# Two feed-forward stages of a two-block layer stack: sums of activations made while gate/up runs, two loads a step, and another sharing out of the norm's work

## The reference

```python
for layer in range(DEPTH):                       # DEPTH = 2
    h = rms_norm(hs, norm_mix_pre[layer])
    mix = pool_mixer(h, ...) if layer < N_A_LAYERS else sliding_window_attention(h, ...)
    hs = hs + rms_norm(mix, norm_mix_post[layer])
    h = rms_norm(hs, norm_ffn_pre[layer])
    gate, up = jnp.split(h @ w_gate_up[layer], 2, axis=-1)
    hs = hs + rms_norm((jax.nn.silu(gate) * up) @ w_down[layer], norm_ffn_post[layer])
# after layer 0: kv_in = rms_norm(hs, kv_norm), keys and values from it
# second_block: h = x * (1 + scale) + shift, then h @ w_in and the rest
```

## Time and profile before

| | us |
|---|---|
| median of 3 runs (range) | 2718.04 (2714.65 to 2721.75) |
| profiled execution | 2723.42 |
| its span | 2721.7 |
| PE busy | 2486.6 (91% of the span) |
| DVE busy | 1529.2 (56%) |
| ACT busy | 1004.8 (37%) |
| POOL busy | 239.8 (9%) |
| f0: down from 569.84 to 823.90, then the norm's rest to | 847.38 |
| f1: down from 1659.65 to 1909.86, then the norm's rest to | 1937.77 |

### The profile page before, as it was taken

How to read it: one execution, slowest core, us unless ns; L and a number is a source line. 1 busy time by engine, 2 the same in 40 slices (tenths; PEclk the granted TensorE clock), 3 DMA queues, 4 the chain that set the end, 5 groups by cost and what they waited for, 6 DMA issues and landing times. The chain is left out here.

```text
span 2721.7 us, 49445 instructions
## 1 busy us (share of the span) xinstructions
PE 2486.6 (91%) x20201; PEld 2066.5 (76%) x20201; DVE 1529.2 (56%) x2352; ACT 1004.8 (37%) x1787; POOL 239.8 (9%) x173
## 2 busy tenths in 40 slices
PE   9899999999977999989999999897799998788778
PEld 7889999987766856667888888685577776677556
DVE  5844454447764558467555554777344563455366
ACT  5433233334444259343323233343221512233231
POOL 2000000001011035100000000002310000222110
PEclk9899999999988999999999999998799999899879
DMA  6423323257444400332222225644212112000132
GB/s 173 118 81 110 108 89 112 97 175 231 138 159 160 186 5 2 101 108 89 82 81 81 81 77 188 236 148 143 97 58 77 39 62 91 4 5 4 57 109 97
DMA packets 122867, 276.15 MB, mean 101 GB/s; under 512 B 17237, under 2 KB 25718, under 8 KB 121150
## 3 DMA queue, kind: packets, MB, share of 16 engines
q1 hardware_dynamic: 122688, 273.60, 30.3%
HBM read 219.68 MB, written 53.28 MB: 100 GB/s over the span
## 5 line engine op out<-in xcount | busy, mean ns | idle before, releaser
L1391 PE MATMUL f1ps<-f1ring 128*128 128x512 f32 x308 | 123.7, 402 | 21.5 <-DVE f1ring L1245 12.9
L1391 PE MATMUL f0ps<-f0ring 128*128 128x512 f32 x308 | 124.9, 406 | 19.3 <-DVE f0ring L1245 13.0
L1392 PE MATMUL f0ps<-f0ring 128*128 128x512 f32 x308 | 122.6, 398 | 0.0
L1393 PE MATMUL f0ps<-f0ring 128*128 128x512 f32 x308 | 122.6, 398 | 0.0
L1392 PE MATMUL f1ps<-f1ring 128*128 128x512 f32 x308 | 122.1, 396 | 0.0
L1393 PE MATMUL f1ps<-f1ring 128*128 128x512 f32 x308 | 122.0, 396 | 0.0
L1287 PE MATMUL f0ps<-b1XH,f0highE 128*128 128x260 f32 x384 | 111.2, 289 | 4.1 <-DVE f0lowE L1112 4.1
L1638 PE MATMUL w_in_b_pr<-b1XH,w_in_b_wH 128*128 128x512 f32 x272 | 110.5, 406 | 3.6 <-DVE w_in_b_wL L1590 3.6
L1169 DVE TENSOR_TENSOR Y_rounded<-Y,Y_rounded 128x1024 fp32r<-128x1024 f32 x80 | 87.1, 1089 | 46.2 <-ACT Y_rounded L971 46.1
L1288 PE MATMUL f0ps<-b1XL,f0highE 128*128 128x260 f32 x384 | 109.6, 285 | 0.0
L1289 PE MATMUL f0ps<-b1XH,f0lowE 128*128 128x260 f32 x384 | 109.6, 285 | 0.0
(11 more groups left out here) (524 smaller groups left out, 7699.4 us busy)
## 6 DMA issues: line engine op xcount, KB each, us to landing
b1XL_plain<-in_w_down SPq DMA_DIRECT2D x66, 256.0 KB, 3.0
residual<-Y SPq DMA_DIRECT2D x32, 512.0 KB, 2.9
Y<-in_w_ada SPq DMA_DIRECT2D x8, 1536.0 KB, 6.5
f0hidden<-f0tm SPq DMA_DIRECT2D x44, 260.0 KB, 4.6
Y<-in_w_gate_up SPq DMA_DIRECT2D x44, 256.0 KB, 2.8
Y<-in_w_gate_up SPq DMA_DIRECT2D x22, 512.0 KB, 3.3
f0ring_plain<-f0hidden SPq DMA_DIRECT2D x44, 256.0 KB, 2.9
f1hidden<-f1tm SPq DMA_DIRECT2D x44, 256.0 KB, 3.0
```

What stands on the lines that cost most here:

```text
L1391: pe.matmul(o, ah, bh, start=fresh, stop=False, skip_group_check=True)
L1392: pe.matmul(o, ah, bl, start=False, stop=False, skip_group_check=True)
L1393: return pe.matmul(o, al, bh, start=False, stop=last, skip_group_check=True)
```

## The change

- **Sums of activations.** While gate/up runs, VectorE makes four sums of the halves of each pair of chunks, and SP stores seven tiles a pair in place of four, each 128x512 (`hidden` now has eight kinds: A11, A12, A22, A21 and SUM1 to SUM4). The pair of plain chunks gets its sums in the down stage: four tiles are loaded back after the last gate/up store, summed before step 9 and stored before step 15.
- **Down.** Every step has exactly two loads. VectorE makes one sum a step in P5, P6, P7 and P4 and none in the others: 44 in place of 88 an FFN. P1 and P5 are rounded in one operation 1024 wide. R is 6, and four steps are loaded before gate/up ends (BEFORE = 4). SP issues step 4's loads behind the store of the last SUM4 (`store_last`), which waits for `pair_last` on VectorE and must have landed.
- **Norm.** VectorE adds the residual behind the multiplication by the gain (L631 after); GpSimd has no part in it. ScalarE issues the stores and the further residual loads (`keep_and_load`). Gains, first weights and first residual tiles are loaded one after the other over steps P6_FIRST + 1 to + 10. A tile's operations come at other steps of P7 and P4. In f1 TensorE turns the residual sum itself, and ScalarE applies scale and shift to the turned tile, eight operations 128x128 with one number per partition for each of both (L596), and then copies the high part (L599).
- **Meta tokens (f0).** They are split over both halves; GpSimd copies them together with four small operations a pair of chunks.

```diff
-    R = 5
+    R = 6
+    BEFORE = 4
...
-                "P1": [(ra, hidden_tiles(j, 0)), (kb, down(j, 0)), (sa, hidden_tiles(j, 1))],
-                "P5": [(sa, hidden_tiles(j, 1)), (ks, hidden_tiles(k2, 1)), (sb, down(j, 1))],
-                "P6": [(sa, down(k2, 1))],
-                "P3": [(ra, hidden_tiles(k2, 0)), (rb, down(k2, 1))],
-                "P7": [(sa, down(j, 0))],
...
+                "P1": [(ca, hidden(A11, j)), (cb, down(low_q, 0))],
+                "P5": [(ca, hidden(SUM1, j)), (rb, down(low_q, 1))],
+                "P6": [(ra, hidden(SUM2, j)), (rb, down(high_q, 1))],
+                "P3": [(ra, hidden(SUM4, j)), (rb, down(high_q, 1))],
+                "P7": [(ra, hidden(SUM3, j)), (rb, down(low_q, 0))],
...
+                def store_last(m):
+                    sp.wait_ge(s["hs"], 4 * m + 4)
+                    sp.dma_start(hidden(SUM4, m + 1), sequence(tm[:, 1, 1])).then_inc(s_ss[2], 16)
...
+                for k, kind in enumerate((A11, A21, A12, A22)):
+                    sp.dma_start(z[:, k], hidden(kind, 0)).then_inc(s_z, 16)
+                store_last(PAIRS - 1)
...
+                for k in range(3):
+                    sp.wait_ge(s_ss[k], 16 * PAIRS)
...
+                def pair_difference(i, m):
+                    dve.wait_ge(s["h"], 2 * i + 6)
+                    dve.tensor_tensor(tm[:, 0, 3], tm[:, 0, 1], tm[:, 0, 2], ALU.subtract).then_inc(s["hs"], 1)
+
+                def pair_sums(i, m):
+                    dve.wait_ge(s["h"], 2 * i + 8)
+                    dve.tensor_tensor(tm[:, 1, 0], tm[:, 0, 2], tm[:, 1, 2], ALU.add).then_inc(s["hs"], 1)
+                    dve.wait_ge(s["hs"], 4 * m + 2)
+                    dve.tensor_tensor(tm[:, 1, 3], tm[:, 1, 0], tm[:, 0, 1], ALU.subtract).then_inc(s["hs"], 1)
+
+                def pair_last(m):
+                    dve.wait_ge(s_st[1][0], 16 * (m + 1))
...
+                    dve.wait_ge(s["hs"], 4 * m + 3)
+                    dve.tensor_tensor(tm[:, 1, 1], tm[:, 1, 1], tm[:, 1, 3], ALU.subtract).then_inc(s["hs"], 1)
...
+                def keep_and_load(t):
+                    tail.keep(act, t)
+                    if t + tail.loads < tail.N:
+                        tail.load(act, t + tail.loads)
...
+                if self.modulate:
+                    for k in range(f.start, f.stop):
+                        act.activation(self.xn[:, t % 2, P * k:P * (k + 1)], self.tp[:, t % self.slots, k, 0:r], ACT.Identity,
+                                       bias=self.shift[:, k:k + 1], scale=self.scale[:, k:k + 1]).then_inc(s["xf"], 1)
+                    act.wait_ge(s["xf"], KC * t + f.stop)
...
-        first_at = {AT + 3 * i: t for i, t in enumerate(TOP)}
-        second_at = {AT + 2 + 3 * i: t for i, t in enumerate(TOP)}
...
+        act_first = {AT + 3 * i: t for i, t in enumerate(TOP)}
+        dve_first = {AT + 1 + 3 * i: t for i, t in enumerate(TOP)}
+        act_second = {AT + 2 + 3 * i: t for i, t in enumerate(TOP)}
+        dve_second = {AT + 3 + 3 * i: t for i, t in enumerate(TOP)}
...
+        load_at = {P6_FIRST + 4 + 2 * t: t for t in range(tail.loads)}
```

More of the change, by code:

```diff
@@ L674, in strassen_ffn @@
     wdn = ins["w_down"][layer]
-    h_out = nc.dram_tensor(name + "hidden", [P, NQ, 2 * half], f32, kind="Internal").ap()
+    h_out = nc.dram_tensor(name + "hidden", [P, 8, HQ, 512], f32, kind="Internal").ap()
+    A11, A12, A22, A21, SUM1, SUM2, SUM3, SUM4 = range(8)
     fetched = 16 * b.fetched
@@ L881, in body @@
                         fetch_down(i + 3, 1)
-                    before = (0 if first else 1 - par)
-                    store(i + 1, before, 0, 2 * (i + 1))
-                    store(i + 1, before, 1, 2 * (i + 1))
+                    if first:
+                        store_classical(1, 0)
+                        store_classical(1, 1)
+                    elif par == 0:
+                        store_odd(i - 1, m - 1)
+                    else:
+                        store_even(i - 1, m)
                     if more:
@@ L889, in body @@
                         fetch_c(i + 4, par)
+                    if par == 0 and not first:
+                        store_last(m - 1)
                 for k in range(2):
@@ L931, in _ @@
-                store(NQ - 1, 1, 0, 2 * NQ - 2)
-                store(NQ - 1, 1, 1, 2 * NQ - 2)
+                body(N - 1, 1, PAIRS - 1, more=False)
                 sp.wait_ge(s["prod"], 7 * N)
-                for par in range(2):
-                    for i in range(2):
-                        sp.wait_ge(s_st[par][i], 16 * (N // 2 + (2 if par == 0 else 0)))
-                if off:
-                    sp.wait_ge(s["meta"], N // 2 + 2)
-                kept = 0
-                for n in range(R - 1, len(steps)):
-                    if n == P6_FIRST - 2:
+                store_odd(N - 1, PAIRS - 1)
@@ L942, in _ @@
+                for n in range(BEFORE, len(steps)):
+                    if n == P1_FIRST + 4:
+                        sp.wait_ge(s["zs"], 4)
+                        for k, kind in ((1, SUM1), (3, SUM2), (4, SUM3), (2, SUM4)):
+                            sp.dma_start(hidden(kind, 0), z[:, k]).then_inc(s_z, 16)
+                    if n == P5_FIRST:
+                        sp.wait_ge(s_z, 128)
+                    step_loads(n)
+                    if n == P6_FIRST + 1:
                         fetch(sp)
+                    if n == P6_FIRST + 2:
@@ L943, in _ @@
                         tail.load_gains(sp)
-                        for t in range(tail.loads):
-                            tail.load(sp, t)
-                    step_loads(n)
-                    if n in keep_at:
-                        tail.keep(sp, kept)
-                        tail.load(sp, kept + tail.loads)
-                        kept += 1
-                for t in range(kept, tail.N):
-                    tail.keep(sp, t)
-                    if t + tail.loads < tail.N:
-                        tail.load(sp, t + tail.loads)
+                    if n in load_at:
+                        tail.load(sp, load_at[n])
@@ L1024, in body @@
                     else:
-                        for n in range(R - 1):
+                        for n in range(BEFORE):
                             step_high(n)
@@ L1077, in _ @@
                 done = {P1_FIRST + AHEAD: (P1_FIRST - 1, bank_b, 0, 0), P6_FIRST + AHEAD: (P6_FIRST - 1, bank_b, 1, 1), P3_FIRST + AHEAD: (P3_FIRST - 1, bank_a, 0, 1)}
-                for n in range(R - 1, len(steps)):
+                for n in range(BEFORE, len(steps)):
                     if n in done:
                         copies(*done[n])
-                    if off and n == R + 2:
+                    if off and n == 7:
                         act.wait_ge(s["meta"], N // 2 + 2)
@@ L1182, in body @@
                     dve.tensor_tensor(tm[:, par, 1], tm[:, par, 1], group(C_GROUP), ALU.add).then_inc(s["c"], 1)
+                    if par == 0 and pair:
+                        pair_last(m - 1)
                     if more:
@@ L1270, in run @@
                         step_low(n)
+                    for n in sorted(low_at):
+                        if n >= len(steps):
+                            tail.vector_low(dve, low_at[n])
                     for k in range(7):
```

319 lines of the change are left out of this document (196 added, 123 removed).

## The result

The changed kernel takes 2675.23 us (median of 4, 2670.3 to 2683.32) against 2717.89: ratio .9845, 95% interval .9816 to .9875. A second set of runs gave 2671.25 against 2722.01, ratio .9816 (.9794 to .9839). So it is 1.5 to 1.8% faster, 43 to 51 us; 2683 was forecast, a gain of 35.

What follows compares the result with a forecast made beforehand. Gate/up was taken as bound by TensorE, down as losing time to stalls in P5, P6, P7 and P4. Terms 0 + 12.4 - 23.7 - 31.0 + 6.8 = -35.5 gave 2683 us, range 2658 to 2707.

Steps and rivals of the forecast that it cites:

- P1: Down product P1 of both FFNs: no change in time, 0 us.
- P7 and P4: Down products beside the norm's operations: fewer PE stalls, -31.0 us, as -14.1 in f0 and -16.9 in f1.
- Gate/up: Gate/up stage: four added VectorE sums a pair of chunks hidden in waits for PE, 0 us; bounds 0 and +56.
- Start of down: P2, down's start: step 4's loads wait for SUM4's store to land, +12.4 us (f1 +7.4, f0 +5.0).
- P5 and P6: Down products P5 and P6: two loads a step, spread burst and fewer sums remove all stalls, -23.7 us.
- Norm behind P4: Norm's rest after P4: +6.8 us, as +6.5 in f0 (addition 4.8, ScalarE's stores 1.7) and +0.3 in f1.
- B: Rival: ScalarE and VectorE in lockstep stall P7 and P4 much as before; +21, 2704 us; chance .16.
- E: Rival: loads late again in P5 to P4, three quarters of 23.7 stays; +18, 2701 us; chance .10.
- D: Rival: gate/up sums wait for a landing and delay PE, or all four are exposed (+56, 2739 us); chance .06.
- C: Rival: the lead swallows the counted waits, boundary stalls and their clock go; 17 less, 2666 us; chance .13.

Runs made afterwards that it cites:

- e2: Changed kernel with step 4 of down loaded ahead of the last SUM4's store, plain pair's tiles behind step 5's loads: P2 37.6 us (f0) and 34.9 (f1).
- e9: Changed kernel with step 4 loaded first, second reciprocal before the addition, SUM4 made earlier and plain pair's tiles loaded one a step: 2653.1 us, ratio .9775.
- e5: Changed kernel with first weights, gains, scale, shift and two residual tiles again issued together before P6: P5 of f1 32.34 us, P5 and P6 of f0 29.92.
- e6: Kernel before the change with, only in f1, the burst of loads spread over several steps, three loads a step kept: P5 of f1 31.8 us, before 41.7.
- e7: Changed kernel with GpSimd adding the residual again in place of VectorE: P7 and P4 76.4 us (f0) and 72.3 (f1), rest of f0 22.9.
- e3: Changed kernel with VectorE's second reciprocal ahead of the residual addition behind the last down step: rest of f0 24.3 us instead of 28.2.
- e12: Changed kernel with SP issuing residual stores and further residual loads in place of ScalarE: P7, P4 and rest 99.0 us in f0, 95.7 in f1.

## Why the prediction was right

The places and the signs were right, and the sum came out 7 us short of the gain: -35.5 against -42.5. The terms were off by +2.1 (start of down), -1.0 (P1), -3.1 (P7 and P4), -4.7 (norm) and -.3 (gate/up).

- **Gate/up at 0**: right, and shown by doubling. The idle time that I read in front of three lines is where the sums went, and more would fit. A pair of chunks takes 38.7 us in the trace, not 42, with 18 us of it idle on VectorE, not 19; this changes nothing in the term.
- **Start of down, +12.4**: +14.5. The mechanism and the landing (+10.5 forecast, +10.7 seen) were right; e2 and e9 took the loss away by order alone. The waits were right in sum: PE's idle time in P2 grew by 3.9 in f0 and 5.1 in f1, where 3.3 and 5.7 were taken. What was too small is the price of the lower clock behind the wait: PE's busy time in P2 grew by 2.7 in each FFN where 1.7 was taken, nearly all of it in step 4, which ran at a granted clock of .50.
- **P5 and P6, -23.7**: right to the tenth, because nothing is left of the stalls, which was the bound taken. For f1, e5 and e6 bear out that the burst was one cause of two, with one correction: the prediction lists its parts as if each had its share, and either of them alone would have done most. In f0, e5 has the burst back and shows no stall, so spreading was not needed there; which of the lighter steps' parts took away f0's 11.9 was not tried.
- **P7 and P4, -31.0**: -34.1. For f0 the sum was right (72.9 against 73.3) by two errors that cancel: PE is idle for 5.6 us and not 7.2, in one wait of 5.2 at P4's start and one of .4, and it is busy for 67.3, where 59.9 + 4.5 + 1.7 = 66.1 were taken. In f1 PE waits 1.7 at P4's start (1.4 forecast), where it was the 8.6 of the earlier trace rows; at P4's last steps it waits 2.7, not 4.8, so there the stall was taken too large. The waits of PE in P7 and P4 of f1 after the change:

```profile
PE f1ps L1515 <- DVE f1ring L1348: 2.7, 1, 2.7
PE f1ps L1515 <- DVE Y L1366: 1.7, 1, 1.7
```

Of the 14.4 and 19.7 us, GpSimd's additions put back cost 3.4 to 4.8 and 3.7 to 3.9, the old steps 1.8 to 3.2 and 3.6 to 3.8, from one execution of each. Each alone leaves most of the gain. Before the change there was one more wait in P7, in front of the turning, in f0 for the low part of a tile ahead and in f1 for the tile that GpSimd had shifted:

```profile
PE f0ps L656 <- DVE b1XL L625: 6.1, 1, 6.1
```

```profile
PE f1ps L656 <- POOL p3xn L552: 6.1, 1, 6.1
```

With GpSimd back it does not return, with the old steps 2.5 us of it in f0 and none in f1: a shorter chain or a later turning suffices against it, and I take this, which no run shows, as why neither experiment gives much back. How the remaining 6 to 12 us divide among the lost scale and shift passes, the single wide rounding of a step in P7 and one ring slot more was not tried and stays open.

- **Norm behind P4, +6.8**: +2.1, the term with the largest error. In f0 the 4.8 for the addition was nearly right: with GpSimd adding again (e7) the norm up to its last high part takes 17.4 in place of 21.8, so 4.4 less, and the order alone (e3) gives 3.1 of it back. The 1.7 for ScalarE's four issues was not there, since they run beside its copies (21.8 in e12 too). In f1 +.3 was forecast and -2.7 measured. Four tiles of 6.1 us in place of 27.9 in all would have been -3.5, so the prediction charged nearly 4 us for a first tile that comes through later. That charge was wrong: the first high part of the rest starts 7.4 us behind P4's end, where it was 7.2. The first high parts before the change, then after:

```profile
1917.09 1.02 ACT L587 ACTIVATE b1XH<-f1ps 128x1024 fp32r<-128x1024 f32 x1 [4.39 <-PE f1ps L656]
1923.81 1.02 ACT L587 ACTIVATE b1XH<-f1ps 128x1024 fp32r<-128x1024 f32 x1 [4.33 <-PE f1ps L656]
```

```profile
1869.71 1.06 ACT L599 ACTIVATE b1XH<-p3xn 128x1024 fp32r<-128x1024 f32 x1
1875.21 1.06 ACT L599 ACTIVATE b1XH<-p3xn 128x1024 fp32r<-128x1024 f32 x1
1879.19 1.06 ACT L599 ACTIVATE b1XH<-p3xn 128x1024 fp32r<-128x1024 f32 x1
```

They follow each other after 5.5 and 4.0 us where it was 6.7 twice, the 4.0 where no square stands between them; 6.1 was taken throughout. The scaled pieces were as taken:

```profile
L596 ACT ACTIVATE p3xn<-f1ps,p3shift,p3scale 128x128 f32<-128x128 f32 x64 | 23.2, 464 | 0.3
```

464 ns each, eight in 2.90 us, so that they start some .35 apart. The Trainium skill (ScalarE: Activation LUTs, What ACT_TABLE_LOAD costs) gives, as an estimate from its figures, 479 ns and .386 apart, 3 and 11% above the trace.
- **Rivals**: B and E did not come; D did not either, and its part about the amount of work is excluded. C, a lead that swallows the waits, is in part what happened in f1.

## What to carry to other kernels

Work given to an engine costs nothing as long as it fits into idle time that stands in front of the same lines in every turn of a loop; read that idle time by line, and double the work to see how much more fits. But look at the last turn: the loop's cover ends there, and here the order of one sum, one store and four loads that were not needed yet cost 5 to 7 us in each FFN. Order the list at such a joint by when each item is needed. Where two causes meet in one stall, undoing each alone tells little of its share; try one in the old kernel and the other in the new. And before a stage of one trace is compared with that of another, see how far it moves between executions in which nothing was changed there: here some moved by 2 us and more.

## What the runs showed that I had not expected

A DMA issued by ScalarE cost its ACTIVATEs nothing that can be seen where a long one stands ahead of it in the program: .33 us of issue inside a copy of 1.15. Behind a root of .29, an issue of .33 and one of .44 put off the next rounding by .7.

The stretch before gate/up of f0 varies by 6 us between executions of the same kernel; in its second 20 us the granted clock was .83 in the profile before and .93 in the one after. PE was busy for all of the 20 us in both, with 135 and 161 matmuls.
